# The inverse of two heads as one block-diagonal matrix in the WKV state stage of an encoder layer

## What is computed

```python
def step(S, inp):
    r_t, w_t, kh_t, ak_t, v_t, kt_t = inp
    sk = jnp.einsum('bhvk,bhk->bhv', S, kh_t)
    S = S * w_t[:, :, None, :] - sk[..., None] * ak_t[:, :, None, :] + v_t[..., None] * kt_t[:, :, None, :]
    return S, jnp.einsum('bhvk,bhk->bhv', S, r_t)
...
o_f = _wkv_scan(..., False)
o_b = _wkv_scan(..., True)
```

## Time and profile before

| | |
|---|---|
| median of 3 runs | 3368.04 us (3367.3 to 3372.46) |
| profiled execution, its own time | 3366.02 us |
| its span | 3364.2 us |
| PE busy | 3225.1 us, 96% of the span |
| PEld, DVE, ACT, POOL busy | 2048.5, 1810.2, 1040.5, 2.5 us |
| mean granted clock of PE | 0.987 of full speed |

### The profile page before, as it was taken

One profiled execution on the slowest core, in us unless ns is written; L12 is line 12 of the kernel. 1 busy time (PEld: TensorE's weight loads), 2 busy tenths in 40 slices (PEclk: granted clock), 3 DMA queues, 4 the chain that ended last, 5 costly groups with the idle time before them and its releaser, 6 DMA issues. The chain is left out here.

```text
span 3364.2 us, 59848 instructions
## 1 busy us (share of the span) xinstructions
PE 3225.1 (96%) x25992; PEld 2048.5 (61%) x25992; DVE 1810.2 (54%) x3002; ACT 1040.5 (31%) x1590; POOL 2.5 (0%) x13
## 2 busy tenths in 40 slices
PE   9999999999999899999999999998999999999997
PEld 4564564554555555577778554565666666666665
DVE  1337762677767579055666332155645445645445
ACT  2336652334334123333434451002321111221111
POOL 0000000000000000000000000000000000000000
PEclk9999999999999999999999999998999999999998
DMA  3221101334534423265654224111212212222211
GB/s 137 58 70 32 45 33 48 121 119 149 184 121 133 176 103 135 106 189 164 172 166 120 91 86 153 61 51 54 65 57 76 69 64 68 69 88 75 69 63 63
DMA packets 218532, 328.51 MB, mean 98 GB/s; under 512 B 55456, under 2 KB 176544, under 8 KB 213152
## 3 DMA queue, kind: packets, MB, share of 16 engines
q1 hardware_dynamic: 218272, 324.69, 29.7%
HBM read 221.74 MB, written 96.34 MB: 95 GB/s over the span
## 5 line engine op out<-in xcount | busy, mean ns | idle before, releaser
L624 PE MATMUL ra_ps<-xT,ring 128*128 128x512 f32 (+1 forms) x1152 | 429.8, 526 | 0.0
L1782 PE MATMUL tl_ps<-merged,pool 128*128 128x320 f32 x1440 | 408.5, 436 | 6.4 <-PEq L108 3.9
L1782 PEld LDWEIGHTS tl_ps<-merged,pool 128*128 128x128 f32 x1440 | 275.6, 192 | 124.6 <-issue 13.1
L624 PEld LDWEIGHTS ra_ps<-xT,ring 128*128 128x128 f32 x1152 | 214.3, 190 | 198.9 <-issue 189.3
L1975 DVE TENSOR_TENSOR oR<-tl_ps,oR 128x320 f32<-128x320 f32 x416 | 202.3, 490 | 150.7 <-PE tl_ps L1782 148.4
L1069 PE MATMUL rg_ps<-xT,ring 128*128 128x512 f32 (+1 forms) x720 | 266.0, 525 | 6.0 <-PEq L108 6.0
L1782 PE MATMUL tl_ps<-tl_Th,pool 128*128 128x320 f32 x720 | 204.1, 435 | 6.1 <-issue 6.1
L1069 PEld LDWEIGHTS rg_ps<-xT,ring 128*128 128x128 f32 x720 | 134.8, 191 | 117.2 <-issue 111.7
L1863 ACT ACTIVATE ring<-tl_ps 128x320 f32<-128x320 f32 x96 | 42.0, 437 | 526.6 <-PE tl_ps L1782 526.6
L1782 PE MATMUL tl_ps<-xT,pool 128*128 128x320 f32 x640 | 183.5, 434 | 0.0
L1981 DVE TENSOR_TENSOR merged<-tl_ps,ring 128x320 f32<-128x320 f32 x96 | 47.2, 492 | 252.8 <-PE tl_ps L1782 135.0
(11 more groups left out here) (241 smaller groups left out, 4639.5 us busy)
## 6 DMA issues: line engine op xcount, KB each, us to landing
pool<-ub SPq DMA_DIRECT2D x320, 160.0 KB, 2.8
ub<-ra_ub SPq DMA_DIRECT2D x32, 1280.0 KB, 5.3
pool<-in_w_ff SPq DMA_DIRECT2D x32, 1024.0 KB, 4.8
pool<-in_w_ff SPq DMA_DIRECT2D x64, 512.0 KB, 3.5
ring<-in_w_in SPq DMA_DIRECT2D x39, 512.0 KB, 3.7
xT<-in_xT SPq DMA_DIRECT2D x16, 640.0 KB, 8.2
ub<-ra_v SPq DMA_DIRECT2D x16, 640.0 KB, 6.8
mg_gate<-gates SPq DMA_DIRECT2D x16, 640.0 KB, 4.0
```

The source lines that it names most:

```text
L624: last = pe.matmul(ps[:, bank + j, 0:n], w[c][:, 128 * i:128 * i + 128], xT[:, i, t0:t0 + n], start=(i == 0), stop=(i == KT - 1))
L1782: last = pe.matmul(bank(n, b), lhs(k), rhs(k), start=(fresh and k == 0), stop=(k == d - 1), skip_group_check=True)
```

## The change

`NF` becomes two buffers, used in turn by even and odd steps, each of 128 partitions by 8 units by 128 columns. The 64 by 64 inverse of head 0 stands at rows and columns 0 to 63, that of head 1 at rows and columns 64 to 127, and the rest is zero. PE then forms U of a unit in one product of the whole array: 128 rows, 128 columns, and 64 moving columns; eight products instead of sixteen. POOL clears both buffers once, and in every step copies the ready 32 by 32 diagonal blocks, in eight copies of 32 partitions; it may start on step g when U of step g - 2 is done. The corners are copied from PSUM: two pieces of 32 partitions by DVE (d = 0), two by ACT (d = 1), after L1342. `own_corners` and the multiplications by `sel` are gone. SP's wait ahead of the loads of `nb` and `rb` is for POOL's copies and the corner product.

```diff
-        NF = st.sb("NF", 128, U, CH)
+        NF = [st.sb(f"NF{i}", 128, U, 2 * CH) for i in range(2)]
...
                 if 0 < m < 8:
-                    sp.wait_ge(nf_done, 16 * m)
+                    sp.wait_ge(nf_own, 32 * m)
+                    sp.wait_ge(n_ready, 4 * m)
                     load_inverse(m + 2, (g + 1) % 4)
...
                 pe.wait_ge(nb_ready[nblk(g) % 3], 64 * (nblk(g) // 3) + 64)
-                if g:
-                    pe.wait_ge(nf_done, 4 * g)
+                after(pe, nf_act, 2 * g)
+                after(pe, nf_dve, 2 * g)
...
                 pe.wait_ge(b_done, g + 1)
-                pe.wait_ge(nf_done, 4 * g + 4)
-                heads(ps, UB, lambda u, h: NF[half(h), u, :], lambda u, h: Bs[half(h), u, :], True).then_inc(u_ready, 1)
+                pe.wait_ge(nf_own, 8 * g + 8)
+                pe.wait_ge(nf_act, 2 * g + 2)
+                pe.wait_ge(nf_dve, 2 * g + 2)
+                for u in range(U):
+                    last = pe.matmul(ps[:, UB, CH * u:CH * u + CH], NF[g % 2][:, u, :], Bs[:, u, :], start=True, stop=True)
+                last.then_inc(u_ready, 1)
...
+        def corner_out(g, d, h):
+
+            o, at = 64 * h + 32 * d, 64 * h + 32 - 32 * d
+            return (NF[g % 2][o:o + 32, 4 * d:4 * d + 4, at:at + 32],
+                    ps[o:o + 32, CB, 256 + 128 * d:384 + 128 * d].rearrange("p (u n) -> p u n", n=32))
...
                 act.activation(Bs[:, :, :], ps[:, BB, :].rearrange("p (u n) -> p u n", n=CH), ACT.Copy).then_inc(b_done, 1)
+                act.wait_ge(n_ready, g + 1)
+                act.wait_ge(nf_zero, 2)
+                after(act, u_ready, g - 1)
+                for h in range(2):
+                    dst, src = corner_out(g, 1, h)
+                    act.activation(dst, src, ACT.Copy).then_inc(nf_act, 1)
...
+            for x in NF:
+                pool.memset(x[:, :, :], 0.0).then_inc(nf_zero, 1)
+            for g in range(NSTEP):
+                n = corners(nb, g)
+                pool.wait_ge(nb_ready[nblk(g) % 3], 64 * (nblk(g) // 3) + 64)
...
+                after(pool, u_ready, g - 1)
+                for d in range(2):
+                    for r in range(0, 128, 32):
+                        pool.tensor_copy(NF[g % 2][r:r + 32, 4 * d:4 * d + 4, r:r + 32], n[d][r:r + 32]).then_inc(nf_own, 1)
...
-            def own_corners(g):
-                n = corners(nb, g)
-                dve.wait_ge(nb_ready[nblk(g) % 3], 64 * (nblk(g) // 3) + 64)
-                if g:
-                    dve.wait_ge(u_ready, g)
-                for d in range(2):
-                    dve.tensor_scalar(NF[:, 4 * d:4 * d + 4, 32 * d:32 * d + 32], n[d], sel[d], None, ALU.mult).then_inc(nf_done, 1)
-
-            def other_corners(g):
-                n = corners(nb, g)
+            def corner_copies(g):
                 dve.wait_ge(n_ready, g + 1)
-                for d in range(2):
-                    us, mine = slice(4 * d, 4 * d + 4), 1 - d
-                    z = ps[:, CB, 256 + 128 * d:384 + 128 * d].rearrange("p (u n) -> p u n", n=32)
-                    dve.scalar_tensor_tensor(NF[:, us, 32 * mine:32 * mine + 32], n[d], sel[mine], z, ALU.mult, ALU.add).then_inc(nf_done, 1)
+                dve.wait_ge(nf_zero, 2)
+                after(dve, u_ready, g - 1)
+                for h in range(2):
+                    dst, src = corner_out(g, 0, h)
+                    dve.tensor_copy(dst, src).then_inc(nf_dve, 1)
```

More of the change, by code:

```diff
@@ L1173, in state_stage @@
         ident64, centre = cst[:, C_ID64:C_ID64 + CH], cst[:, C_CEN:C_CEN + CH]
-        sel = [cst[:, C_SEL + i:C_SEL + i + 1] for i in range(2)]
         nb_ready = st.sems("nb_ready0 nb_ready1 nb_ready2")
-        set_up, sc_ready, masked, kt_done, v_ready, v_done, x_ready, w_done, n_ready, nf_done = st.sems(
-            "set_up sc_ready masked kt_done v_ready v_done x_ready w_done n_ready nf_done")
+        set_up, sc_ready, masked, kt_done, v_ready, v_done, x_ready, w_done, n_ready = st.sems(
+            "set_up sc_ready masked kt_done v_ready v_done x_ready w_done n_ready")
+        nf_zero, nf_own, nf_act, nf_dve = st.sems("nf_zero nf_own nf_act nf_dve")
         bd_ready, b_ready, b_done, u_ready, u_done, s_ready, t_done, s_done, o_ready, o_done = st.sems(
@@ L1405, in _ @@
                 pool.tensor_copy(ub[i][:, :, 5 * CH:6 * CH], ident64.unsqueeze(1).broadcast_to([128, U, CH])).then_inc(set_up, 1)
+            for x in NF:
[3 more added lines that the diff above has]
+                pool.wait_ge(nb_ready[nblk(g) % 3], 64 * (nblk(g) // 3) + 64)
+                if g == 0:
+                    pool.wait_ge(nf_zero, 2)
+                after(pool, u_ready, g - 1)
+                for d in range(2):
+                    for r in range(0, 128, 32):
+                        pool.tensor_copy(NF[g % 2][r:r + 32, 4 * d:4 * d + 4, r:r + 32], n[d][r:r + 32]).then_inc(nf_own, 1)
         @block.vector
@@ L1469, in _ @@
             for g in range(NSTEP):
-                own_corners(g)
                 if g + 1 < NSTEP:
@@ L1473, in _ @@
                     mask(g + 1, 1)
-                other_corners(g)
+                corner_copies(g)
                 if g + 1 < NSTEP:
```

## The result

The changed kernel takes 3392.27 us (median of 6 runs, 3387.93 to 3396.88), the kernel before 3367.67 us (6 runs, 3358.70 to 3372.46): 1.0077 times the time, with an interval of 1.0067 to 1.0087. That is +24.6 us. Forecast were 3385 us, a range of 3369 to 3399, and a chance of 0.80 for slower.

What follows compares the result with a forecast made beforehand. The state stage was taken as bound by PE and, nearly as hard, by its instruction supply. Product U +30.8, corners +4 and supply -16 made +18.8 us on 3366.0: 3385 us, range 3369 to 3399.

Steps and rivals of the forecast that it cites:

- The product U: U on PE: 16 whole-array loads 0.11 us apart, 1.70 us instead of 0.93; +30.8 us in 40 steps.
- The corners: Ahead of U: ACT's two corner copies end after its copy of B and delay U; +4 us (0 to 7).
- The supply: PE's instruction fetch: fewer instructions and longer steps shrink PE's idle holes; -16 us.
- The first rival, Fast whole-array loads: At U: 128-column loads come about 0.07 us apart, product stays near 0.93 us; -8 us, 3358 us, chance 0.10.
- The forecast's bounds: Low and high sums of the whole forecast: +3 and +32 us, 3369 to 3398 us.
- the ends of the product: U on PE with load gaps of 0.07 or 0.16 us: +7 or +61 us.
- The supply gives everything back: PE's instruction fetch: the longer step leaves no idle hole at all; +3 us, 3369 us, chance 0.08.
- Load and streaming in turn: At U: loads and streaming do not overlap, gap 0.16 us; +45 us, 3411 us, chance 0.04.
- POOL as the bound: POOL's eight diagonal-block copies a step take over 1.3 us each; at 1.5, +64 us, 3430 us, chance 0.03.

Runs made afterwards that it cites:

- u_cols64: Changed kernel with U as sixteen products of 128 rows by 64 columns, two column halves side by side; 3374.01 us, 1.0016 times the kernel before.
- u_stream112: Changed kernel with 112 instead of 64 moving columns in each of U's eight products (result partly wrong); 3387.49 us, 1.0067 times the kernel before.
- one_head: Kernel before with U's eight products of the second head left out (half the result wrong), 32 instructions fewer a step; 3360.27 us, ratio 0.9991.
- waits_swapped: Changed kernel with PE's last two waits ahead of U exchanged, DVE's corners first and ACT's last; 3389.78 us, 1.0077 times the kernel before.
- u_tiled: Changed kernel with U again as sixteen 64 by 64 products, read from the new buffers; 3376.25 us, 1.0026 times the kernel before.
- cols64_swapped: Changed kernel with U as sixteen products of 128 rows by 64 columns and PE's wait for ACT's corners last; 3369.36 us, ratio 1.0014 to before.
- before_wide: Kernel before with only U changed, to eight whole-array products using two old units' blocks as weights (wrong result); 3391.47 us, ratio 1.0075.
- u_pairs128: Kernel before with U's sixteen 64 by 64 products streaming 128 instead of 64 columns (result partly wrong); 3385.68 us, 1.0067 times the kernel before.
- scores_256: Kernel before with 256 instead of 192 moving columns in each scores product, same result and instruction count; 3368.64 us, 1.0008 times the kernel before.

## Why the prediction was right, and where its terms were off

The time lay in the range and on the side forecast, 7.3 us above the number; as a difference, 24.6 us came where 18.8 were forecast. The mechanism was the one forecast too: a longer product, partly given back by the supply of instructions. That the number came so near has some luck in it, since three terms were off by 3 to 5 us, in both directions. The mean step, which was to be near 11.0 us, is 11.30 in the profiled execution. Term by term:

**The product U** was forecast at 15 x 0.11 + 0.05 = 1.70 us instead of 0.93. It is 1.69, with gaps of 0.111. The row that carried it, two whole-array loads in 0.30 us, was the right one, and that of the transposes the wrong one. The columns alone set it (`u_cols64`), and not the streaming (`u_stream112`). The Trainium skill (TensorE: Matmul & The Clock Gate, "LDWEIGHTS (loading the stationary operand)") gives a load its columns over 1.2 in ns, whatever its rows: 107 ns here. The distances between the starts of loads agree with it: 0.111 us at 128 columns, and 0.89 / 15 = 0.06 at 64 where they have no partner (`one_head`). The duration that the profile gives a load, 0.19 us, is longer. One thing was missed: the last matmul lasts 0.275 us instead of 0.22, and the scores behind it start 0.06 later. In full the term is 0.82 us a step, 33 us instead of 30.8.

**The corners** were forecast at 0.10 us a step, +4 (0 to 7). ACT's lateness was foreseen: copies of 0.27 us each, ending behind B as worked out. The term is mis-sized by what followed. I let U's load follow 0.12 us after ACT; it follows after 0.22, since the wait for DVE stands behind the wait for ACT (`waits_swapped` takes 0.11 off). A clean step so starts U 0.29 us later. Over the 40 steps the time from the last scores matmul to U sums to 27.0 us instead of 19.0, so the term is 8 us. `u_tiled` and `u_cols64`, which have this term almost alone, are 8.1 and 5.9 over before. With the waits swapped and U short, `cols64_swapped` is 4.3 over.

**The clock** is the term that the sum did not have. In the profiled execution 24 us of the stage's 40 steps are at the lower level, 3 us before. At 3.1 us for 6.8 that is some 9 us lost. That execution was one of the slower ones; over all of them the mean clock is 0.9860 against 0.9877, which makes 4.5 us by the 2.65 us for 0.001.

**The supply** was forecast at -16 us. The clean step grew by 1.10 us (9.51 to 10.61), and the mean step by 0.78. So what a mean step has above a clean one fell from 1.01 to 0.69 us: -0.32 x 40 = -13 us. The list of "issue" agrees, 27.8 to 14.6 against the 12 that were forecast. But the 0.69 us hold the clock's loss, so the supply gave back more than 13. `before_wide` has the long product alone: 33 us of work, some 14 us over before without its clock, so about 19 us came back. Two kernels show the parts: 33 - 22 = 11 us by the longer step (`u_pairs128`), and some 9 us by fewer instructions (`one_head`). All these are estimates. So the size was near, but in part by luck, since the working behind it was wrong on one point. It took the relief as a matter of blocks per us, the same wherever the time is added. By that working, `scores_256` was to be 25 over before and was 4.2, and `u_pairs128` should have been about the same and was 20.6. The relief depends on where in the step the time is put. The waits ahead of U itself went first, all 8.3 us of them. The first rival had them go because the program becomes thinner there; they went as well in `u_pairs128`, to 1.3 us, with no instruction fewer. Those at L1342, two groups ahead, kept 6.7 of 9.6 us.

**Together**, between the profiled executions: 33 + 8 + 9 - 19 = +31 us, against 29.3. Between the medians: 33 + 8 + 4.5 - 19 = +26.5, against 24.6. The corners and the clock, 4 and 4.5 us more than forecast, are in part made good by the 3 us more of the supply.

The forecast's bounds have a slip. The upper one takes -6 us for the supply, where its ends are given as -1.4 and -28, and neither bound holds the ends of the product, +7 and +61 us. With the gap at 0.11 this did no harm.

**The rivals.** Fast whole-array loads: out, the gap is 0.111. The supply gives everything back: 14.6 us of "issue" are left. Load and streaming in turn: out, streaming 48 columns more moves the loads by nothing. The Trainium skill (same page, "The mechanism" in Part 3) has the rule that a load overlaps only with matmuls of other row groups. Here it and the measurement differ, and the measurement decides: whole-array loads start 0.111 us apart beside 112 columns of streaming. The same section also lets a load be pulled ahead when it goes to a background weight buffer, and that would allow what is seen here; the prediction left this out. POOL as the bound: its copies are 0.29 us, not 1.3, and hidden.

**What stays open.** Why the loads of the transposes of the earlier trace rows come 0.07 us apart where those of a product need 0.11: no kernel here tried it. It is also open what makes the clock dip more often in some kernels, and which blocks of instructions gain when time is added at one place. A version with one corner engine and one wait only was not tried.

## What to carry to other kernels

A block-diagonal matrix halves the instructions but not the weights' columns: each load has twice as many, and can no longer run beside its partner in another quarter of the array. With 64 moving columns the product was bound by its loads, so it nearly doubled; count gaps between loads first, and streaming second.

Where PE's own instructions are the second bound, ask where in the program added or saved time falls, not only how much: some 31 us of extra streaming cost 4 us when they were spread over the step, 21 in one place. Compare the mean clocks of the executions, too, before a difference of a few us is put down to the code: here 0.001 stood for 2.65 us. And of several waits in a row, put the one that is met last at the end.

## What the runs showed of the hardware

- A wait that was met long ago still takes 0.11 us when it stands behind a late one on PE: U's load came 0.22 us after the late engine with it, 0.11 without.
- Loads of whole-array products pay for columns, not rows: 0.138 us for 64 columns with 128 rows, 0.192 for 128 columns; at 128 columns they start 0.111 us apart, whether 64 or 112 columns stream beside them.
- PE's program came in packets of 16 KB (1.57 MB in 96), never less than 3.2 us apart in any kernel here. All waits of PE put down to "issue" in the even part, 355 in 14 profiles, ended 1.0 to 1.6 us after the end of such a packet.
- PE's granted clock fell to the lower level within the stage in kernels whose PE was just as busy by the count: means of 0.96 to 0.99 with wide loads and 64 moving columns, 1.00 with the same loads and 112 columns, 1.00 with pairs of 128. But `one_head`, with narrow loads, had 0.97 too, so wide loads are not the whole of it; what makes the clock fall is not shown.
- A dip of 6.8 us at the lower level made a step 3.1 us longer (13.7 instead of 10.6), and 0.001 less mean clock went with 2.65 us more over 137 executions.
- Loads of 64 columns in one quarter of the array start 0.06 us apart (`one_head`), and so do pairs of them in two quarters.
- Copies of 32 partitions by 128 elements take 0.27 us on ACT and 0.28 on DVE, both from PSUM, and 0.29 on POOL.
